# Routing of a top-2-of-8 expert layer: another operand held in the router and in the row selection, and the row scale and bias applied inside the expert items

## The chip, the cores and the metric

The kernel runs on one core of one Trainium2 chip. The metric is the device time of one execution in microseconds (us). TensorE (PE), VectorE (DVE), ScalarE (ACT), GpSimd (POOL) and the DMA queues of SyncE (SP), ACT and POOL are written by hand, engine by engine, and are held in order by semaphores alone.

## What is computed

Two batches of 256 tokens with 1024 channels go through two encoder layers with shared weights. Each layer is a token mixer, a layer norm, a channel mixer and another layer norm. The channel mixer of the second layer is the one that matters here:

```
x = layer_norm(ALPHA * x + mix, ln1_g, ln1_b)
logits = x @ w_router + b_router            # 8 experts
top_v, top_i = lax.top_k(logits, 2)
top_w = softmax(top_v)
f = sum over the two experts e:  top_w[e] * (silu(x @ w_g[e]) * (x @ w_u[e])) @ w_d[e]
x = layer_norm(ALPHA * x + f, ln2_g, ln2_b)
```

All arithmetic is float32. A float32 product is made of three products of rounded parts: high by high, high by low, low by high. The parts are tiles such as `ewhi` and `ewlo`; ACT rounds the high part and DVE subtracts it from the raw value to get the low one.

## The kernel before, in words

The 512 tokens are four tiles of 128 rows, `X[:, tt, :]`. In `out_rows(2, ...)` DVE closes the layer norm of the token mixer tile by tile: residual, statistics, `rstd` by ACT (L506), reciprocal, and the normalisation at L852, which counts `ln_norm`. Rows are normalised there, but the norm's scale and bias (`lngb`) are not applied yet.

**Routing.** PE turns the tiles to features by channel, two tiles at a time (`transposes(3)`, L1266). ACT (`xt_full`, L539) and DVE (L1003) move them to `xt32` and apply scale and bias by channel; each has half of the eight channel blocks of each half of the tokens. The router (L1476) holds 128 channels by 128 tokens of `xt32` and streams the 8 columns of the router weights `wrt`, 32 products. Beside that the rows themselves get scale and bias: POOL (`affine`, L1178, L1179) for tiles 0 and 1, DVE (`row_affine`, L816, L814) for tiles 2 and 3. ACT then rounds the rows to `xrh` (L686), DVE makes `xrl` (`x_low`, L1012).

DVE takes the logits (L1028), finds the two best experts, makes the 0/1 table `both`; PE counts places in each expert's queue (L1483 to L1486); DVE makes `sel` (L1055), a 0/1 matrix that picks the 128 rows of the first item, then the rows' places in memory `ridx` (L1071) and the list of items `tab` (L1080). POOL scatters the rows to memory by `ridx` (L1231, eight indirect DMAs), and multiplies `X` by ALPHA for the residual (L1237).

**Items.** An item is up to 128 rows of one expert; there are 11. Its weights come as 17 pieces of 1 MB (two of 0.75 MB) through a ring of six raw slots `eraw`. Fifteen of the pieces are split by ACT (`e_split`, L697) and DVE (`e_low`, L1019) into three slots of `ewhi` and `ewlo`; SP loads a slot again once `e_low` has read it. Pieces 0 to 10 make gate and up (`hidden_tanh` on ACT, `hidden_rows` on DVE L1099 and L1103, `hidden_features` on PE L1521, `hidden_high` and `hidden_low`), pieces 11 to 16 the way down. The first item's rows never go through memory: 64 products (L1496) of a 128 by 128 block of `xrh` or `xrl`, held, with the 128 columns of `sel` give them as features at once. ACT (`xg_high`, L715) and DVE (`xg_low`, L1092) split these to `xgh` and `xgl`. Later items load their rows from memory (`load_rows`, L706, which waits until all rows are scattered) and PE turns them (L1509). Within an item ACT's order around this is: split of the next item's piece 0, `xg_high`, `y_out(0)`, splits of its pieces 1 and 2, `y_out(1)`, the store of the results. Every loop runs all its engines through the same 11 items.

At the end POOL gathers the two results of each row, DVE adds them to `X` (L1138) and the last norm closes.

Of the kernel before, what the change touches and what calls it, by code (L numbers as in the profile page):

```python
# [25 lines left out]
F32 = mybir.dt.float32  # L26
# [8 lines left out]
P = 128  # L35
# [103 lines left out]
def build_trunk(nc, x0, x1, dense_w, expert_gu, expert_dn, consts, slots, vecs, mix, lnrow, wr, br, xd, yd, y0, y1):  # L139
    ctx = ExitStack()  # L140
    with ctx:
# [91 lines left out]
        slot_no = at("slot_no", [P, CAP], F32)  # L233
        assert here() <= nc.sbuf_usable_end, here()
# [8 lines left out]
        top[0] = o_xth + 2 * KD * TOK * 4  # L243
        lg = at("lg", [P, TT, NE], F32)
# [76 lines left out]
        x_scaled = sem("x_scaled")  # L321
# [79 lines left out]
        def _(sp):  # L401
# [13 lines left out]
            def ln_rows(n):  # L415

                if n == 3:
                    sp.wait_ge(x_affine_v, TT + 2)
                    sp.wait_ge(x_affine, TT + 2)
                elif n == 2:  # L420
# [36 lines left out]
            for p in range(NPC):  # L457
# [3 lines left out]
                if p == ERING - 1:  # L461
                    sp.dma_start(slot_no[:, :], slots).then_inc(in_slots, 16)
                    ln_rows(3)
# [27 lines left out]
        def _(act):  # L491
# [42 lines left out]
            def xt_full():  # L534

                for h in range(2):
                    for k in (0, 1, 4, 5):
                        act.wait_ge(xt_tr, n_tr(3, h, k))
                        nc.scalar.activation(xt32[:, k, h * SEQ:(h + 1) * SEQ], xt_bank(3, h, k), ACT.Identity,  # L539
                                             scale=vcol(1, V_L1G + k), bias=vcol(1, V_L1B + k)).then_inc(xt_full_a, 1)  # L540
# [96 lines left out]
            for L in range(DEPTH):  # L637
# [43 lines left out]
            for tt in range(TT):  # L681
                if tt < 2:
                    act.wait_ge(x_affine, TT + tt + 1)
                else:
                    act.wait_ge(x_affine_v, TT + tt - 1)
# [13 lines left out]
            for o in range(ESPL):  # L699
                e_split(o, 0)  # L700
# [38 lines left out]

            xg_high(0)  # L740
# [39 lines left out]
        def _(dve):  # L780
# [217 lines left out]
            for i, c in enumerate((C_ONE, C_TRI)):  # L998
                V.tensor_copy(ones16[:, i, :], cst[:, c:c + P])
            for h in range(2):  # L1000
                for k in (2, 3, 6, 7):
                    dve.wait_ge(xt_tr, n_tr(3, h, k))
                    V.tensor_scalar(xt32[:, k, h * SEQ:(h + 1) * SEQ], xt_bank(3, h, k), vcol(1, V_L1G + k),  # L1003
# [649 lines left out]
```

## Time and profile before

| | us |
|---|---|
| median of 3 runs (1688.52 to 1689.79) | 1689.69 |
| the profiled execution | 1689.56 |
| its span, first to last instruction | 1687.7 |
| PE busy in the span | 1598.7 (95%) |
| DVE busy | 1157.8 (69%) |
| ACT busy | 774.9 (46%) |
| POOL busy | 198.4 (12%) |

The span has three parts: dense work to 1036 us; the routing from there to the first product of the first item at 1082.94 us; then the items and the closing norm. The page's line of slices shows DMA engines at 9 tenths or more in nearly every slice of the items and at 1 to 5 tenths in most slices before them.

### The profile page before, as it was taken

What the parts mean: (1) busy time and instruction counts of PE and PEld (TensorE: products, weight loads), DVE (VectorE), ACT (ScalarE), POOL (GpSimd) and SP (SyncE); (2) the same over time, 40 slices, a digit from 0 to 9 for tenths busy, and PEclk for the clock granted to TensorE, in tenths of its full rate; (3) what the DMA queues carried; (4) which work ended last, traced back from release to release, by engine and by line L of the source; (5) the groups of instructions that cost most, each with busy time, mean ns of one, the idle gap of its engine ahead of it and who ended that gap; (6) DMA issues with size and microseconds to landing.
All of it is one profiled execution on the core that took longest, in us unless ns stands there. A gap on an engine that the chain in (4) does not pass through costs nothing.

```text
span 1687.7 us, 20082 instructions
## 1 busy us (share of the span) xinstructions
PE 1598.7 (95%) x7383; PEld 1282.7 (76%) x7383; DVE 1157.8 (69%) x1312; ACT 774.9 (46%) x990; POOL 198.4 (12%) x122
## 2 busy tenths in 40 slices
PE   7999999999999999999999998899999999999990
PEld 6877778888888888887777787777777777777770
DVE  6888747584444423579886667678877788877786
ACT  5344442252222222444443422366766667666661
POOL 0400006060000000005000242400000000000006
PEclk9999999999999999999999998699999999999995
DMA  5232222225454332222122342689999999999994
GB/s 205 75 100 75 75 101 92 95 84 199 167 184 141 115 100 97 76 88 99 67 73 77 111 150 89 230 298 357 384 357 352 354 358 354 385 351 348 353 341 162
DMA packets 134381, 325.71 MB, mean 193 GB/s; under 512 B 7984, under 2 KB 19632, under 8 KB 133808
## 3 DMA queue, kind: packets, MB, share of 16 engines
q1 hardware_dynamic: 125584, 292.36, 49.2%
q0 software_dynamic: 5296, 19.92, 3.0%
q10 hardware_dynamic: 3440, 12.58, 1.9%
q8 instruction: 41, 0.67, 0.2%
q14 instruction: 20, 0.16, 0.0%
HBM read 300.20 MB, written 24.64 MB: 192 GB/s over the span
## 4 chain that ended last, share of the span: by engine, by line
PE 73%; DMA 13%; DVE 6%; ACT 4%; issue 4%; ACTq 0%; SPq 0%; POOL 0%; DVEq 0%
PE bank L1273 15%; PE bank L1274 14%; PE bank L1275 14%; DMA eraw<-expert_gu 12%; PE bank L1312 4%; PE bank L1311 4%; PE bank L1313 4%; PE bank L1542 3%; PE bank L1544 3%; PE bank L1543 3%; ACT ewhi L697 3%; PE bank L1549 2%; DVE ewlo L1019 2%; PE bank L1385 1%; PE bank L1398 1%
## 5 line engine op out<-in xcount | busy, mean ns | idle before, releaser
L1019 DVE TENSOR_TENSOR ewlo<-eraw,ewhi 128x2048 fp32r<-128x2048 f32 x168 | 384.8, 2291 | 115.0 <-ACT ewhi L697 114.9
L1273 PE MATMUL bank<-xth,whi 128*128 128x512 f32 (+1 forms) x976 | 381.3, 391 | 1.9 <-DVE wlo L788 1.9
L788 DVE TENSOR_TENSOR wlo<-raw,whi 128x1024 fp32r<-128x1024 f32 x170 | 239.1, 1410 | 207.4 <-ACT whi L501 207.1
L697 ACT ACTIVATE ewhi<-eraw 128x2048 fp32r<-128x2048 f32 x168 | 321.7, 1916 | 122.2 <-DMA eraw<-expert_gu 73.5
L1274 PE MATMUL bank<-xtl,whi 128*128 128x512 f32 (+1 forms) x976 | 370.7, 380 | 0.0
L1275 PE MATMUL bank<-xth,wlo 128*128 128x512 f32 (+1 forms) x976 | 370.5, 380 | 0.0
L501 ACT ACTIVATE whi<-raw 128x1024 fp32r<-128x1024 f32 x170 | 178.5, 1051 | 137.1 <-PE bank L1313 123.9
L1273 PEld LDWEIGHTS bank<-xth,whi 128*128 128x128 f32 x976 | 184.1, 189 | 50.8 <-issue 8.5
L1274 PEld LDWEIGHTS bank<-xtl,whi 128*128 128x128 f32 x976 | 184.1, 189 | 36.6 <-issue 3.8
L1275 PEld LDWEIGHTS bank<-xth,wlo 128*128 128x128 f32 x976 | 184.0, 189 | 35.2
L1542 PE MATMUL bank<-ewhi,xgh 128*128 128x512 f32 (+1 forms) x528 | 205.3, 389 | 1.6 <-DVE xgl L1092 1.6
L1544 PE MATMUL bank<-ewhi,xgl 128*128 128x512 f32 (+1 forms) x528 | 197.2, 373 | 0.0
L1543 PE MATMUL bank<-ewlo,xgh 128*128 128x512 f32 (+1 forms) x528 | 196.8, 373 | 0.0
L1542 PEld LDWEIGHTS bank<-ewhi,xgh 128*128 128x128 f32 x528 | 99.9, 189 | 20.1 <-issue 4.2
L1543 PEld LDWEIGHTS bank<-ewlo,xgh 128*128 128x128 f32 x528 | 100.0, 189 | 18.7 <-issue 2.4
L1544 PEld LDWEIGHTS bank<-ewhi,xgl 128*128 128x128 f32 x528 | 99.7, 189 | 18.1
L876 DVE SCALAR_TENSOR_TENSOR cv<-hpad,vec,cv 128x512 f32<-128x512 f32 x120 | 89.9, 750 | 3.1
L562 ACT ACTIVATE gates<-bank,hvec 128x512 f32<-128x512 f32 x48 | 33.0, 688 | 126.2 <-PE bank L1275 126.2
L1542 PE MATMUL bank<-ewhi,hth 128*128 128x512 f32 x176 | 75.4, 429 | 0.0
L1241 POOL DMA_INDIRECT yg<-item_results,ridx x8 | 8.4, 1044 | 551.5 <-ACTq L767 549.3
L1220 POOL TENSOR_TENSOR mrg<-mrg 128x512 f32<-128x512 f32 x16 | 27.7, 1734 | 362.0 <-DVE mrg L973 362.0
L1544 PE MATMUL bank<-ewhi,htl 128*128 128x512 f32 x176 | 68.9, 391 | 0.0
(226 smaller groups left out, 2223.1 us busy)
## 6 DMA issues: line engine op xcount, KB each, us to landing
eraw<-expert_gu SPq DMA_DIRECT2D x124, 1024.0 KB, 9.2
raw<-dense_w SPq DMA_DIRECT2D x170, 512.0 KB, 3.4
eraw<-expert_dn SPq DMA_DIRECT2D x44, 1024.0 KB, 11.1
eraw<-expert_dn SPq DMA_DIRECT2D x22, 768.0 KB, 10.1
item_rows<-zero POOLq DMA_DIRECT2D x8, 1024.0 KB, 4.8
rows<-item_rows ACTq DMA_DIRECT2D x11, 512.0 KB, 6.8
item_results<-yrows ACTq DMA_DIRECT2D x11, 512.0 KB, 7.8
lngb<-lnrow SPq DMA_DIRECT2D x4, 1024.0 KB, 5.2
```

Source lines behind the costliest of these rows:

```text
L501: nc.scalar.activation(whi[:, g % SPL, :], raw[:, g % RAW, :], ACT.Copy).then_inc(hi_done, 1)
L697: nc.scalar.activation(ewhi[:, o % ESPL, 0:n], eraw[:, p % ERING, 0:n], ACT.Copy).then_inc(e_hi, 1)
L788: V.tensor_tensor(wlo[:, g % SPL, :], raw[:, g % RAW, :], whi[:, g % SPL, :], ALU.subtract).then_inc(lo_done, 1)
L876: ins = V.scalar_tensor_tensor(acc, src, w, acc, ALU.mult, ALU.add)
L1019: V.tensor_tensor(ewlo[:, o % ESPL, 0:n], eraw[:, p % ERING, 0:n], ewhi[:, o % ESPL, 0:n], ALU.subtract).then_inc(e_lo, 1)
L1273: mm(out, wh, xh, start=first, stop=False)
L1274: mm(out, wh, xl, start=False, stop=False)
L1275: return mm(out, wl, xh, start=False, stop=last)
L1311: mm(out, ah[:, k, t], wh, start=(k == 0), stop=False)
L1542: mm(out, ah[:, k, :], wh, start=(k == 0), stop=False)
L1543: mm(out, ah[:, k, :], wl, start=False, stop=False)
L1544: ins = mm(out, al[:, k, :], wh, start=False, stop=(k == last - 1))
```

## The change: what it does

1. **Router.** The 8 columns of `wrt` are held and 256 tokens of `xt32` are streamed, 16 products. The logits lie with experts on partitions, ACT copies them to SBUF (`lgt`), and four PE transposes turn them. ACT moves all eight channel blocks of the first token half and four of the second; DVE four of the second.
2. **Rows.** No row gets scale and bias before the items. `xrh`, `xrl` and the scattered rows are the normalised rows. POOL's `affine` and DVE's `row_affine` of this norm are gone, and POOL's multiplication by ALPHA.
3. **Selection.** `sel` is held and 512 columns of `xrh` and `xrl` are streamed, 16 products, which give the first item's rows as rows. ACT copies them to `rows`, and PE turns them as in the later items.
4. **Scale and bias** come back in `xg_high`, in every item: eight activations of 128 by 128 to a new tile `xg32`, then the rounding from there.
5. **Residual base.** ALPHA times scale and bias of `X` is done on DVE, eight operations of 128 by 1024, inside the first item, which DVE now has ahead of its loop.
6. **Order on DVE.** All of `x_low` stands before the logits; of the first three `e_low` one stands after `tab` and before `ridx`, two after `xg_low(0)`.
7. The last norm's `lngb` is loaded by POOL once the residual base is done.

```diff
-                    ln_sqrt(2)
-                    xt_full()
+                    ln_sqrt(2, range(TT - 1))
+                    xt_full(0, (0, 1, 2))
+                    ln_sqrt(2, (TT - 1,))
+                    xt_full(0, (3, 4, 5, 6, 7))
+                    xt_full(1, (0, 1, 4, 5))
...
+            e_split(0, 0)
+            act.wait_ge(rt_logit, 1)
+            nc.scalar.activation(lgt[0:NE, :], bank[0][0:NE, :], ACT.Copy).then_inc(rt_lgt, 1)
...
             def xg_high(j):
+                if not isinstance(j, int):
+                    act.wait_ge(xg_lo, j * 2)
                 for q in range(2):
                     act.wait_ge(rows_tr, j * 2 + (q + 1))
-                    nc.scalar.activation(xgh[:, 4 * q:4 * q + 4, :], quarters(bank[B_XG[q]][:, :]),
+                    for k in range(4 * q, 4 * q + 4):
+                        last = nc.scalar.activation(xg32[:, k, :], bank[B_XG[q]][:, (k % 4) * CAP:(k % 4 + 1) * CAP],
+                                                    ACT.Identity, scale=vcol(1, V_L1G + k), bias=vcol(1, V_L1B + k))
+                    last.then_inc(xg_full, 1)
+                    act.wait_ge(xg_full, j * 2 + (q + 1))
+                    nc.scalar.activation(xgh[:, 4 * q:4 * q + 4, :], xg32[:, 4 * q:4 * q + 4, :],
                                          ACT.Copy).then_inc(xg_hi, 1)
...
+            for c in range(2):
+                act.wait_ge(sel_mm, c + 1)
+                nc.scalar.activation(rows[:, 512 * c:512 * c + 512], bank[B_Y[c]][:, :], ACT.Copy).then_inc(rows_own, 1)
             xg_high(0)
...
+            def residual_base(i):
+                tt, part = i // 2, i % 2
+                if i == 0:
+                    dve.wait_ge(scattered, 16 * 2 * TT)
...
+                if part == 0:
+                    step(V.scalar_tensor_tensor(x, x, ALPHA, lngb[:, 0, :], ALU.mult, ALU.mult))
+                else:
+                    V.scalar_tensor_tensor(x, lngb[:, 1, :], ALPHA, x, ALU.mult, ALU.add).then_inc(x_base, 1)
...
+            def item(j, first=False):
                 for p in range(N_GUP):
                     if p % 2 == 1 or p == 10:
                         hidden_rows(p // 2, j)
                     if p % 2 == 0 and 2 <= p < 10:
                         hidden_low(p // 2 - 1, j)
                     e_low(p + ESPL, j)
+                    if first and p >= 6:
+                        residual_base(p - 6)
                 e_low(14, j)
+                if first:
+                    for i in range(5, 8):
+                        residual_base(i)
                 e_low(0, j + 1)
                 xg_low(j + 1)
...
             transposes(3)
+            for h in range(2):
+                pe.wait_ge(xt_full_a, (8, 12)[h])
+                if h == 1:
+                    pe.wait_ge(xt_full_b, 4)
+                cols = slice(h * SEQ, (h + 1) * SEQ)
+                for k in range(KD):
+                    ins = mm(bank[0][0:NE, cols], wrt[:, k, :], xt32[:, k, cols], start=(k == 0), stop=(k == KD - 1))
+            ins.then_inc(rt_logit, 1)
+            pe.wait_ge(rt_lgt, 1)
             for tt in range(TT):
-                for k in range(KD):
-                    ins = mm(bank[0][:, tt * NE:(tt + 1) * NE], xt32[:, k, tt * P:(tt + 1) * P], wrt[:, k, :],
-                             start=(k == 0), stop=(k == KD - 1))
+                ins = nc.tensor.transpose(bank[1][:, tt * NE:(tt + 1) * NE], lgt[0:NE, tt * P:(tt + 1) * P],
+                                          cst[0:NE, C_ID:C_ID + NE])
...
-            for k in range(KD):
+            for c in range(2):
                 for tt in range(TT):
                     for part in (xrh, xrl):
-                        ins = mm(bank[B_XG[k // 4]][:, (k % 4) * CAP:(k % 4 + 1) * CAP], part[:, tt, k * P:(k + 1) * P],
-                                 sel[:, tt, :], start=(tt == 0 and part is xrh), stop=(tt == TT - 1 and part is xrl))
-                if k % 4 == 3:
-                    ins.then_inc(rows_tr, 1)
+                        ins = mm(bank[B_Y[c]][:, :], sel[:, tt, :], part[:, tt, 512 * c:512 * c + 512],
+                                 start=(tt == 0 and part is xrh), stop=(tt == TT - 1 and part is xrl))
+                ins.then_inc(sel_mm, 1)
...
+            pe.wait_ge(rows_own, 2)
+            turn_rows()
```

The order of DVE's instructions shows points 2 and 6. First the kernel before, from the casts of two constant tiles (`ones`) to the table of the two best experts (`pick`); then the changed kernel, from the same moves to `xt` on.

```order
L999 CAST ones_126<-cst 128x128 x2
L1003 TENSOR_SCALAR xt_64<-bank,vec 128x256 x8
L816 TENSOR_TENSOR X<-X,lngb 128x1024
L814 TENSOR_TENSOR X<-X,lngb 128x1024
L816 TENSOR_TENSOR X<-X,lngb 128x1024
L814 TENSOR_TENSOR X<-X,lngb 128x1024
L1012 TENSOR_TENSOR xrl<-X,xrh 128x1024 x2
L1019 TENSOR_TENSOR ewlo<-eraw,ewhi 128x2048 x2
L1028 TENSOR_TENSOR lg<-brt,bank 128x32
```

```order
L1013 TENSOR_SCALAR xt_64<-bank,vec 128x256 x4
L1018 TENSOR_TENSOR xrl<-X,xrh 128x1024 x4
L1031 CAST ones_128<-cst 128x128 x2
L1034 TENSOR_TENSOR lg<-brt,bank 128x32
L1037 MAX mx_110<-lg 128x8 x4
```

Ahead of the logits (`lg`) four row operations, four moves to `xt` and two low parts of weights are gone, and two more `xrl` stand there; the casts stand behind them.

In the first item DVE of the changed kernel has the residual base between the low parts of the weights (`ewlo`) and the hidden blocks (`eb`, `eh`):

```order
L1025 TENSOR_TENSOR ewlo<-eraw,ewhi 128x2048
L1103 SCALAR_TENSOR_TENSOR X<-X,lngb 128x1024
L1111 SCALAR_TENSOR_TENSOR eb<-eb,bank 128x256
L1115 SCALAR_TENSOR_TENSOR eh<-eb,bank 128x256
L1025 TENSOR_TENSOR ewlo<-eraw,ewhi 128x2048
L1105 SCALAR_TENSOR_TENSOR X<-lngb,X 128x1024
L1120 TENSOR_TENSOR htl<-bank,hth 128x256
L1025 TENSOR_TENSOR ewlo<-eraw,ewhi 128x2048
L1103 SCALAR_TENSOR_TENSOR X<-X,lngb 128x1024
L1111 SCALAR_TENSOR_TENSOR eb<-eb,bank 128x256
```

The rows with `X` are new there; three of them stand ahead of the fifth hidden block and five ahead of the sixth.

On ACT the changed kernel has, from the splits of the first pieces to the end of the first item's input:

```order
L697 ACTIVATE ewhi<-eraw 128x2048
L701 ACTIVATE lgt<-bank 8x512
L697 ACTIVATE ewhi<-eraw 128x2048 x2
L706 ACT_TABLE_LOAD
L706 ACTIVATE etmp<-etmp 128x4
L752 ACTIVATE rows<-bank 128x512 x2
L721 ACTIVATE xg_104<-bank,vec 128x128 x4
L725 ACTIVATE xgh<-xg_104 128x512
L721 ACTIVATE xg_104<-bank,vec 128x128 x4
L725 ACTIVATE xgh<-xg_104 128x512
```

Before, the two `xgh` stood alone behind `etmp`, each read from PSUM; the copies to `rows`, the `xg_104` (the tile `xg32`) and the copy to `lgt` are new.

## Rows read from the trace of the kernel before

**Rows 1.** Busy time by window: us, PE, PEld, DVE, ACT, POOL, PE clock, DMA share, GB/s.
```profile
1056.00:1126.00 70.00, 62.18 (x296) 52.95 (x296) 50.34 (x83) 35.60 (x33) 21.49 (x12) 0.79 0.71 250
...
1096.00:1106.00 10.00, 9.95 (x45) 7.68 (x44) 9.80 (x9) 7.59 (x8) 4.28 (x2) 1.00 1.02 380
...
1156.00:1606.00 450.00, 435.97 (x1970) 337.15 (x1969) 358.67 (x290) 302.09 (x274) 0.00 (x0) 1.00 0.98 359
```

**Rows 2.** One window of the selection with PE alone: us, PE, clock, DMA share, GB/s.
```profile
1070.00:1072.00 2.00, 2.00 (x12) 0.50 0.29 119
```

**Rows 3.** Timeline of PE in the routing: start, us, instruction, idle before and its releaser.
```profile
1036.07 1.91 PE L1266 MATMUL bank<-cst,X 128*128 128x128 f32 x16
1041.07 3.39 PE L1266 MATMUL bank<-cst,X 128*128 128x128 f32 x16 [3.09 <-DVE X L852]
1047.57 13.18 PE L1476 MATMUL bank<-wrt,xt 128*128 128x8 f32 x64 [3.12 <-DVE xt L1003]
...
1063.85 0.25 PE L1486 MATMUL bank<-both,ones 128*128 128x8 bf16 x4
...
1082.94 0.79 PE L1542 MATMUL bank<-ewhi,xgh 128*128 128x512 f32 x1 [1.63 <-DVE xgl L1092]
```

**Rows 4.** Chain that ended last, routing and second item: start, us, what.
```profile
1067.43 13.90 PE bank L1496 x64
...
1083.73 0.43 PE bank L1543
...
1174.09 2.59 PE bank L1549 x6
```

**Rows 5.** Timeline of DVE, routing and first item.
```profile
1040.94 4.68 DVE L999 CAST ones<-cst 128x128 bf16<-128x128 f32 x2
...
1061.35 0.18 DVE L1028 TENSOR_TENSOR lg<-brt,bank 128x32 f32<-128x32 f32 x1
...
1063.61 2.35 DVE L1012 TENSOR_TENSOR xrl<-X,xrh 128x1024 fp32r<-128x1024 f32 x2
...
1066.17 1.11 DVE L1055 TENSOR_SCALAR sel<-slot_no,pos,both 128x128 fp32r<-128x128 f32 x4
...
1070.58 2.28 DVE L1019 TENSOR_TENSOR ewlo<-eraw,ewhi 128x2048 fp32r<-128x2048 f32 x1
...
1089.26 2.29 DVE L1019 TENSOR_TENSOR ewlo<-eraw,ewhi 128x2048 fp32r<-128x2048 f32 x1 [6.59 <-ACT ewhi L697]
```

**Rows 6.** Timeline of ACT, routing and first item (ACTq: its DMA queue).
```profile
1038.82 1.92 ACT L539 ACTIVATE xt<-bank,vec 128x256 f32<-128x256 f32 x4
...
1051.66 1.06 ACT L686 ACTIVATE xrh<-X 128x1024 fp32r<-128x1024 f32 x1 [2.62 <-DVE X L814]
...
1081.35 0.60 ACT L715 ACTIVATE xgh<-bank 128x512 fp32r<-128x512 f32 x1 [6.23 <-PE bank L1496]
...
1095.92 0.38 ACTq L706 DMA_DIRECT2D rows<-item_rows  x1
```

**Rows 7.** Timeline of ACT, end of the second item.
```profile
1182.14 1.91 ACT L697 ACTIVATE ewhi<-eraw 128x2048 fp32r<-128x2048 f32 x1 [2.46 <-PE bank L1544]
1184.85 1.92 ACT L697 ACTIVATE ewhi<-eraw 128x2048 fp32r<-128x2048 f32 x1 [0.80 <-DMA eraw<-expert_gu]
```

**Rows 8.** Single lines over the whole run: durations in ns min/median/max, first and last start.
```profile
L852 DVE TENSOR_SCALAR X<-X,mv,rstd x12: 811/814/1866, 331.9 to 1039.1; 128x1024 f32<-128x1024 f32 x12
...
L1138 DVE SCALAR_TENSOR_TENSOR X<-yg,mixk,X x8: 1285/1285/3245, 1656.7 to 1674.4; 128x1024 f32<-128x1024 f32 x8
...
L730 ACT ACTIVATE ht<-bank x22: 253/310/370, 1118.4 to 1632.8; 128x256 f32<-128x256 f32 x11, 128x128 f32<-128x128 f32 x11
...
L1509 PE MATMUL bank<-cst,rows x88: 270/272/273, 1122.1 to 1633.2; 128*128 128x128 f32 x88
```

**Rows 9.** The scatters on POOL: the line, and the instruction that waits for them.
```profile
L1231 POOL DMA_INDIRECT item_rows<-X,ridx x8: 947/952/2545, 1069.8 to 1080.3; - x8
...
1088.11 12.17 POOL L1237 TENSOR_SCALAR X<-X 128x1024 f32<-128x1024 f32 x4 [6.86 <-DMA item_rows<-X,ridx]
```

More of the change, by code:

```diff
@@ L243, in build_trunk @@
         top[0] = o_xth + 2 * KD * TOK * 4
+        lgt = at("lgt", [P, TOK], F32)
         lg = at("lg", [P, TT, NE], F32)
@@ L532, in xt_evac, with xt_full @@
                             nc.scalar.activation(xth[:, k, cols], xs[:, i % 4, :], ACT.Copy).then_inc(xt_hi, 1)
[L534 to L540, printed above, removed]
+            def xt_full(h, ks):
+                for k in ks:
+                    act.wait_ge(xt_tr, n_tr(3, h, k))
+                    nc.scalar.activation(xt32[:, k, h * SEQ:(h + 1) * SEQ], xt_bank(3, h, k), ACT.Identity,
+                                         scale=vcol(1, V_L1G + k), bias=vcol(1, V_L1B + k)).then_inc(xt_full_a, 1)
             def proj_out(L, m):
@@ L1080, in _ @@
             V.tensor_copy(tab[:, :], tabf[:, :]).then_inc(rt_tab, 1)
-            e_low(2, 0)
+            e_low(0, 0)
+            step(V.scalar_tensor_tensor(row[:, :, :], begin.unsqueeze(1).broadcast_to([P, TT, NE]), float(CAP),
+                                        pos[:, :, :], ALU.mult, ALU.add))
+            for k in range(2):
+                step(V.tensor_tensor(rtmp[:, :, :], row[:, :, :], pick[:, k], ALU.mult))
+                step(V.tensor_reduce(rowk[:, k, :], rtmp[:, :, :], AX.X, ALU.add))
+            V.tensor_copy(ridx[:, :, :], rowk[:, :, :]).then_inc(rt_row, 1)
             dve.wait_ge(rt_e, 1)
@@ L1113, in _ @@
             turns = dve.value_load(tab[0:1, 16:17], min_val=NE, max_val=MAX_ITEMS)
-            xg_low(0)
-            with dve.Fori(0, turns) as j:
+            def item(j, first=False):
                 for p in range(N_GUP):
@@ L1126, in _ @@
                 e_low(2, j + 1)
+            xg_low(0)
+            e_low(1, 0)
+            e_low(2, 0)
+            item(0, True)
+            with dve.Fori(1, turns) as j:
+                item(j)
             final = sem("final_step")
@@ L1232, in _ @@
                         ap=ridx[:, k, tt:tt + 1], axis=0), in_=X[:, tt, :], in_offset=None).then_inc(scattered, 16)
-            pool.wait_ge(scattered, 16 * 2 * TT)
-            pool.wait_ge(xr_lo, TT)
-            for tt in range(TT):
-                G.tensor_scalar(X[:, tt, :], X[:, tt, :], ALPHA, None, ALU.mult).then_inc(x_scaled, 1)
+            pool.wait_ge(x_base, TT)
+            pool.dma_start(lngb[:, :, :], lnrow[3:4].broadcast_to([P, 2, D])).then_inc(in_ln3, 16)
             pool.wait_ge(all_stored, 1)
@@ L1507, in rows_to_features @@
                     pe.wait_ge(rows_in, j * 16 + 16)
-                    for k in range(KD):
-                        ins = nc.tensor.transpose(bank[B_XG[k // 4]][:, (k % 4) * P:(k % 4 + 1) * P],
-                                                  rows[:, k * P:(k + 1) * P], ident)
-                        if k % 4 == 3:
-                            ins.then_inc(rows_tr, 1)
+                    pe.wait_ge(xg_full, j * 2 + 2)
+                    turn_rows()
                 def hidden_features(b):
```

89 lines of the change are left out of this document (37 added, 52 removed).

## The prediction

> **What bounds the kernel now.** I read the windows first, to see where time can be won at all. From 1156 to 1606 us the DMA engines are busy 0.98 of the time and PE 436 of 450 us [rows 1]: the items run at the pace at which weights arrive and are used. The turning of the rows (L1509), 8 per item, goes from 1122.1 to 1633.2 us in 11 items [rows 8], so ten steps of about 51 us. Nothing in the change makes an item lighter; an earlier first item moves all that follows by the same amount, a later one too. From 1056 to 1126 us the DMA engines are busy only 0.71 [rows 1], so some 20 us of transfer time lie unused there, and an earlier start finds room.
>
> The timeline of PE then gives the stage that the change rebuilds: 1036.07 us (first tiles turned) to 1082.94 us (first product of the first item), with holes of 3 us before the second half of the tiles, before the router and after it [rows 3]. The chain that ended last runs through DVE's casts and row operations, the logits, and the 64 selection products, 13.90 us [rows 4]. These are all at half clock: the granted clock is 0.50 (1.2 GHz) in a window in which PE never stopped [rows 2].
>
> **The new path, step by step**, to the new start of the first item.
>
> *Second half of the tiles.* The norm of tile 3 begins at 1039.15 us and takes 1.87 us; the others take 0.81 [rows 8]. POOL multiplies rows at that moment, which is gone afterwards, so I take 0.81: PE turns tiles 2 and 3 from 1040.0 instead of 1041.07. That takes 1.91 us (first half, full clock) or 3.39 (second half, half clock) [rows 3]; I take 1.91, as the hole before it shrinks from 3.1 to 2.0 us: 1041.9.
>
> *Router.* ACT now moves eight blocks of the first half, at 0.48 us each [rows 6]: three before the last `rstd`, five behind it from 1038.9, so to 1041.3. The other eight are shared with DVE and are ready while PE does the first half. The price of 16 products of 256 float32 columns is not in the trace; the nearest row is three of 512 float32 columns in 2.59 us at full clock [rows 4], 0.43 for 256, so 6.9 us in all at full and 13.8 at half clock. I take 7.7, two of them at half clock, since these are streamed columns and not 8-column products: the end is 1049.6. The old router took 13.18 us [rows 3] and ended at 1060.75.
>
> *Logits.* The copy to `lgt` is taken as the 0.60 us of a 512-column PSUM read on ACT [rows 6]; four transposes at 0.2 us (half clock, 3.39 over 16), handoffs 0.1: logits start at 1051.1. ACT is there in time: four `xrh` at 1.06 us [rows 6] and one split at 1.92 [rows 7] end near 1049.2. DVE's four `xrl` (2.35 us per two) end at 1049.1. The two casts behind them took 4.68 us before [rows 5], beside POOL; with POOL idle I take 0.4, and keep 2.7 us (their end at 1053.8) for the range.
>
> *Selection matrix.* From the logits to the end of `sel` it was 1061.35 to 1067.28 us. In it the two `xrl` run 1063.61 to 1065.96 [rows 5] while the counts are ready at 1064.10 [rows 3]. They now stand earlier, so 1.86 us go: 4.1 instead of 5.9, and the selection starts at 1055.4.
>
> *Selection.* 16 products of 512 columns at 0.43 us (half clock, first products of the first item [rows 4]) are 6.9 us, at full clock half that. In the first item the clock rose after six such products. I take 5.3, bounds 3.5 and 6.9. End: 1060.7.
>
> *From there to the first item.* Before: `xgh` 0.60, `xgl` and handoff 1.0 [rows 3, 6]. Now a copy to `rows` 0.65, four transposes 0.6, eight activations, two roundings of 0.6, handoffs 0.2, then the same 1.0. One activation of 128 columns: 0.48 for 256 [rows 6] less the 0.12 by which a copy of 128 is shorter than one of 256 (253 and 370 ns [rows 8]), 0.36, so 2.9. Together 6.5: **the first item starts at 1067.2 instead of 1082.94, 15.7 us earlier.**
>
> **What the first item gives back.** DVE is busy 9.80 of 10 us there [rows 1], so what is added cannot lie in holes. The two `e_low` that move behind `xg_low(0)` (2 x 2.29) fit the 6.59 us that DVE idles at the item's start [rows 5]. The eight operations of the residual base are taken as L1138, the same operation and size: 1.30 us with handoff [rows 8]. Three stand ahead of the fifth hidden block and five ahead of the sixth, and PE needs both before it can turn them and go on: 6.5 us. DVE runs ahead of PE by 1.7 us: the first low part ends at 1091.55 [rows 5], and PE can use it only after 36 products, from 1093.2. So 4.8 us stay. Bounds: nothing, if DVE can catch up in time, and all eight, 10.4 us. The last three lie where DVE waits for weights (358.67 of 450 us busy in the steady items [rows 1]).
>
> **Every later item** costs ACT 3.0 us more (eight activations and handoffs). It stands ahead of the splits of pieces 1 and 2, before which ACT idles 2.46 and 0.80 us [rows 7], 3.26 together; the second ends by a DMA. So nothing, but with 0.3 us to spare. The scale and bias rows that POOL and DVE lost were on the chain and are counted above; the multiplication by ALPHA on POOL ran beside the first item and is worth nothing. The load of the last `lngb` moves from SP to POOL's queue, with the whole of the items to land.
>
> **Sum:** -15.7 + 4.8 = -10.9 us against the profiled 1689.56 us (the median is 1689.69): **1678.7 us**.
>
> **Rivals.**
> *Scatters.* They started 13.1 us ahead of the first item and had landed 18.3 us after their start [rows 9]; `load_rows` follows 13.0 us into the item [rows 6]. By the order above they now start near 1061.2, 6.0 us ahead, and land 12.3 us into it: just in time. One of the eight took 2.55 us where the median is 0.95 [rows 9], and a low part of weights ran on DVE then. If three meet one, they land 4.1 us late for ACT, of which PE has about 1 us in hand: 3.1 us more, 1681.8. The Trainium skill, "SBUF — State Buffer", section "Who interferes with whom", has a DVE operation with two SBUF inputs contend with a POOL operation that reads SBUF, but finds descriptor generation not held up by such an operation; by that this rival costs nothing, and the row of 2.55 us speaks against it.
> *The residual base in full*, 10.4 us: 1684.3. For it: DVE's 9.80 of 10 us. *Swallowed*: 1673.9.
> *Half clock throughout.* The router ends at 1043.4 + 13.8 = 1057.2, 7.6 us later, and the selection takes 1.6 more: 1687.9, no change that a measurement tells. For it: back-to-back products did not lift the clock before [rows 2]; against it, products of 512 columns did, within the first item. The Trainium skill, "TensorE: Matmul & The Clock Gate", section "What's actually happening", has sustained activity lift the clock; by that alone the old selection would have run at full clock, which the 0.50 contradicts.
> *The stream sets the end*, whatever the first item does: 1689.6. Against it the 20 us of unused DMA time, more than 10.9.
> *Longer items: slower.* If an activation of `xg32` costs more than 0.40 us, the splits behind come late and with them the next loads, in ten items. At 0.53 us the gain of 10.9 is used up; at 0.60, 4.9 us per item, it is 1.6 x 10 - 10.9 = 5 us slower, about 1695. Against it: 0.36 as worked out, and PE needs pieces 1 and 2 later than ACT ends them.
>
> **How the numbers follow.** Forecast 0.50; scatters 0.15; residual in full 0.12; swallowed 0.12; half clock 0.04; stream 0.03; longer items 0.04. A measurement of this kernel tells about 0.2%, 3.4 us, from no change. The first four are faster by more than that: 0.89; half clock and stream 0.07; slower 0.04. The range goes from the case of nothing given back, 1673.5, to the residual in full with 1 us more, 1685.5, which also takes in casts that stay slow (2.7) and a selection at half clock (1.6) beside the forecast.
>
> **What would show it.** Right: the router as 16 products in 7 to 9 us, the selection in about 5, the first product of the first item near 1067, turnings of rows (L1527 now) first 44 us behind it instead of 39, then 51 us apart, DVE without a hole in the middle of the first item, PE idle there before the fifth and sixth hidden blocks. Wrong: ACT waiting for the scatters before its load of rows; steps between the items above 51 us; products of 0.86 us in the whole router; a first item that begins after 1072.

## The result, and the profile after

The changed kernel takes **1680.48 us** (median of 5 runs, 1678.43 to 1682.19) against 1689.5 us (5 runs, 1688.52 to 1689.79) for the kernel before on the same chip: ratio 0.9949, 95% interval 0.9937 to 0.996. It is faster by about 9 us; 1678.7 was forecast, and the range of 1673.5 to 1685.5 holds the result. The profiled execution, the fastest of the five, took 1678.43 us; its span is 1676.6 us.

Two windows of the changed kernel, the first item and the steady items (us, then busy time of PE, PEld, DVE, ACT and POOL, PE clock, DMA share, GB/s), answer to [rows 1]:

```profile
1056.00:1126.00 70.00, 60.71 (x259) 46.74 (x258) 55.54 (x54) 41.47 (x50) 10.75 (x9) 0.94 0.82 299
1156.00:1606.00 450.00, 436.51 (x1963) 336.72 (x1963) 359.00 (x291) 328.48 (x346) 0.00 (x0) 1.00 0.98 359
```

The steady stage is what it was: the DMA engines at 0.98, the same 359 GB/s. ACT does 26.4 us more there, its eight activations per item, and PE does not notice. The first window now has more weights in it (299 GB/s, 250 before), as the items start earlier.

The timeline of PE answers to [rows 3]:

```profile
1033.99 1.91 PE L1285 MATMUL bank<-cst,X 128*128 128x128 f32 x16
1037.95 1.97 PE L1285 MATMUL bank<-cst,X 128*128 128x128 f32 x16 [2.05 <-DVE X L865]
1039.84 7.07 PE L1496 MATMUL bank<-xt,wrt 128*8 128x256 f32 x32
1047.59 0.41 PE L1500 MATMUL bank<-cst,lgt 8*128 8x8 f32 x4 [0.68 <-ACT lgt L701]
...
1052.37 0.77 PE L1520 MATMUL bank<-xrh,sel 128*128 128x512 f32 x1 [1.60 <-DVE sel L1057]
...
1058.45 0.39 PE L1520 MATMUL bank<-xrl,sel 128*128 128x512 f32 x1
1059.53 1.09 PE L1527 MATMUL bank<-cst,rows 128*128 128x128 f32 x8 [0.69 <-ACT rows L752]
1065.57 0.79 PE L1573 MATMUL bank<-ewhi,xgh 128*128 128x512 f32 x1 [4.95 <-DVE xgl L1092]
```

This execution came to the first row 2.08 us earlier than the profiled one before (1036.07). The routing has no part in that: the issues of the third `lngb` load, 90 us ahead of it, already stand 1.94 us apart (944.05 here, 945.99 before). In the eleven later runs the first row lies between 1034.72 and 1035.90; why all twelve come there earlier than the one trace of the kernel before, by 1.1 us on average, is open. So I count from that row. From there to the first product of the first item it was 46.87 us and is **31.58 us, 15.3 us less**; from that product to the turning of the second item's rows it was 39.2 us and is **44.69 us, 5.5 us more**; the ten steps between turnings took 510.3 us and take 511.7, **1.4 more**; and from the last turning to the end it is 54.6 us instead of 55.3. The last turning of the kernel before, then two of the changed kernel, that of the third item's rows and the last:

```profile
1632.42 1.04 PE L1509 MATMUL bank<-cst,rows 128*128 128x128 f32 x8
```

```profile
1162.99 1.03 PE L1527 MATMUL bank<-cst,rows 128*128 128x128 f32 x8
...
1621.98 1.03 PE L1527 MATMUL bank<-cst,rows 128*128 128x128 f32 x8
```

Together -15.3 + 5.5 + 1.4 - 0.7 = -9.1 us; the medians differ by 9.0. That they agree so closely is partly luck. In this execution the second half of the tiles and the router ran at full clock. In six of the ten later traces with the same code up to there they did so only in part, and the selection begins 20.0 us after the first row instead of 18.4. PE in the same window of the changed kernel, then of the run with the residual spread (us, busy, granted clock, DMA share, GB/s):

```profile
1040.00:1046.80 6.80, 6.80 (x32) 1.00 0.00 0
```

```profile
1040.00:1046.80 6.80, 6.80 (x31) 0.75 0.00 0
```

Where the first item gives time back is seen in PE's next rows:

```profile
1095.50 0.43 PE L1552 MATMUL bank<-cst,eh 128*128 128x128 f32 x2 [1.26 <-DVE eh L1115]
...
1103.42 0.43 PE L1552 MATMUL bank<-cst,eh 128*128 128x128 f32 x2 [1.86 <-DVE eh L1115]
...
1107.27 0.33 PE L1552 MATMUL bank<-cst,eh 128*128 128x128 f32 x1 [0.53 <-DVE eh L1115]
...
1110.26 1.03 PE L1527 MATMUL bank<-cst,rows 128*128 128x128 f32 x8
```

DVE makes the hidden blocks late, three times, 3.65 us in all, and here is what stands ahead of them (DVE, with two rows of the routing):

```profile
1046.47 0.35 DVE L1031 CAST ones<-cst 128x128 bf16<-128x128 f32 x2
1048.04 0.19 DVE L1034 TENSOR_TENSOR lg<-brt,bank 128x32 f32<-128x32 f32 x1 [1.21 <-PE bank L1500]
...
1093.24 1.22 DVE L1103 SCALAR_TENSOR_TENSOR X<-X,lngb 128x1024 f32<-128x1024 f32 x1
1094.50 0.42 DVE L1111 SCALAR_TENSOR_TENSOR eb<-eb,bank 128x256 f32<-128x256 f32 x1
1094.95 0.42 DVE L1115 SCALAR_TENSOR_TENSOR eh<-eb,bank 128x256 f32<-128x256 f32 x1
...
1097.49 1.22 DVE L1105 SCALAR_TENSOR_TENSOR X<-lngb,X 128x1024 f32<-128x1024 f32 x1
...
1101.16 1.22 DVE L1103 SCALAR_TENSOR_TENSOR X<-X,lngb 128x1024 f32<-128x1024 f32 x1
...
1105.41 1.22 DVE L1105 SCALAR_TENSOR_TENSOR X<-lngb,X 128x1024 f32<-128x1024 f32 x1
1106.55 0.28 DVE L1111 SCALAR_TENSOR_TENSOR eb<-eb,bank 128x128 f32<-128x128 f32 x1
...
1109.26 1.22 DVE L1103 SCALAR_TENSOR_TENSOR X<-X,lngb 128x1024 f32<-128x1024 f32 x1
```

One operation of the residual base is 1.22 us. One stands ahead of the fourth hidden block, three ahead of the fifth and four ahead of the sixth (1106.55); the fifth operation (1109.26) comes behind it, where the section on the change and the prediction count it in front. The other part is the clock. Windows of PE alone (us, busy, granted clock, DMA share, GB/s): the selection, the way from it to the first item, the first item's start and what follows:

```profile
1052.40:1056.40 4.00, 4.00 (x10) 0.50 0.00 0
...
1060.00:1065.00 5.00, 0.62 (x6) 0.97 1.03 413
1066.00:1071.00 5.00, 5.00 (x13) 0.50 0.96 307
1072.00:1074.00 2.00, 2.00 (x11) 1.00 0.95 328
```

The selection begins at half clock (1.2 GHz) and reaches the full one only for its last products. Then PE is busy 0.62 of 5 us, while ACT scales the first item's input, and the item begins at half clock again: some 13 products, 5.7 us, pass before the rise. In the kernel before it was six. The forecast had some half-clock products in the selection, too few, and none at the item's start beyond those of the kernel before.

### The profile page after: what moved, and what is told of

The parts are those of the page before. It is cut to its first block, busy times and chain, and to the rows that moved or that the text cites. A ratio compares the mean times of both kernels' runs of the same rounds, so it can differ in the third digit from the quotient of the medians.

```text
span 1676.6 us, 20036 instructions
## 1 busy us (share of the span) xinstructions
PE 1584.8 (95%) x7315; PEld 1261.0 (75%) x7315; DVE 1156.1 (69%) x1312; ACT 813.8 (49%) x1093; POOL 177.5 (11%) x115
## 4 chain that ended last, share of the span: by engine, by line
PE 72%; DMA 13%; DVE 6%; ACT 4%; issue 4%; ACTq 0%; SPq 0%; POOL 0%; DVEq 0%
PE bank L1292 15%; PE bank L1293 14%; PE bank L1294 14%; DMA eraw<-expert_gu 11%; PE bank L1331 4%; PE bank L1330 4%; PE bank L1332 4%; PE bank L1573 3%; PE bank L1575 3%; PE bank L1574 3%; ACT ewhi L697 3%; PE bank L1580 2%; DVE ewlo L1025 2%; PE bank L1404 1%; PE bank L1417 1%
## 5 line engine op out<-in xcount | busy, mean ns | idle before, releaser
L1575 PEld LDWEIGHTS bank<-ewhi,xgl 128*128 128x128 f32 x528 | 100.1, 190 | 18.4
L1574 PE MATMUL bank<-ewlo,hth 128*128 128x512 f32 x176 | 68.7, 390 | 0.0
L1332 PE MATMUL bank<-whi,hl 128*128 128x512 f32 x176 | 68.5, 389 | 0.0
```

Source lines behind the costliest of these rows:

```text
L1332: return mm(out, al[:, k, t], wh, start=False, stop=(k == 2 * per - 1))
L1574: mm(out, ah[:, k, :], wl, start=False, stop=False)
L1575: ins = mm(out, al[:, k, :], wh, start=False, stop=(k == last - 1))
```

## The experiments

My theory after this: the give-back is the residual base (about 4 us) and the clock (1 to 2 us). Rivals: the scatters, ACT's eight activations, DVE's loop.

| run | median us | ratio to the kernel before |
|---|---|---|
| no residual base | 1671.52 (one run) | |
| residual spread | 1675.36 | 0.9923 (0.9909 to 0.9937) |
| PE kept busy | 1681.37 | 0.9962 (0.9948 to 0.9976) |
| no scale and bias in the items | 1683.96 (one run) | |
| old router | 1684.97 (one run) | |
| old selection | 1683.78 (one run) | |
| PE kept busy, rows loaded later | 1676.26 | 0.993 (0.9913 to 0.9946) |
| the same, residual spread | 1671.78 | 0.9904 (0.9887 to 0.992) |
| changed kernel, `lngb` loaded last | 1677.83 | 0.9938 (0.9925 to 0.9952) |
| all four together | 1670.19 | 0.9891 (0.9876 to 0.9906) |
| all four, scaling shared with DVE | 1670.34 | 0.9893 (0.9878 to 0.9909) |

The changed kernel itself stands at 0.9949 (0.9937 to 0.996). Where a run's interval overlaps with that, what tells the two apart is their traces, one of each.

**Without the residual base.** ALPHA, scale and bias of the residual are left out. The load of the last `lngb`, which had waited for them, then goes once all scatters have landed, in the first item.

```diff
-                    if first and p >= 6:
-                        residual_base(p - 6)
...
-                if first:
-                    for i in range(5, 8):
-                        residual_base(i)
...
-            pool.wait_ge(x_base, TT)
+            pool.wait_ge(scattered, 16 * 2 * TT)
+            pool.wait_ge(in_ln, 16 * 3)
```

> Leaves out the residual's ALPHA, scale and bias (eight operations on DVE in the first item). In the changed kernel the first item takes 44.7 us from its first product to the turning of the next rows, 39.2 before. Theory: 3.7 of the 5.5 us are PE waiting for hidden blocks behind the residual base on DVE (1.26, 1.86 and 0.53 us before L1552), the rest is half clock at the start of the item. Then this kernel shows 41.0 us, none of these three waits, and about 3.7 us less in all. Rival: the two low parts of weights that moved behind the first item's input, or the later loads, hold the item; then it stays at 44 to 45 us.

The first product of the first item begins at 1065.75 us; PE's rows behind it:

```profile
1088.43 0.43 PE L1547 MATMUL bank<-cst,eh 128*128 128x128 f32 x2 [0.21 <-DVE eh L1115]
...
1106.21 1.03 PE L1522 MATMUL bank<-cst,rows 128*128 128x128 f32 x8
```

40.46 us from first product to turning, 4.2 less than 44.69, and of the three waits one of 0.21 us is left. The residual base costs 4.2 us. What remains over the 39.2 us of the kernel before, 1.3 us, is there without it. The whole fell by more than the 3.7 us expected: the median by 9.0, the span of the profiled execution by 6.9, of which 2.9 are the ten steps (508.85 us instead of 511.72). In this run POOL issues the `lngb` load at 1080.30, not at 1116.64.

**Residual spread** over the first four items, two operations each, at their ends.

```diff
-                    if first and p >= 6:
-                        residual_base(p - 6)
...
-                    for i in range(5, 8):
-                        residual_base(i)
+                    residual_base(2 * j)
...
+                    residual_base(2 * j + 1)
...
-            item(0, True)
-            with dve.Fori(1, turns) as j:
+            for i in range(TT):
+                item(i, True)
+            with dve.Fori(TT, turns) as j:
```

> The same eight operations, two in each of the first four items, where DVE waits for ACT in every item (before the low part of the next item's piece 0, and behind the low parts of its input). Theory: these holes, 2.5 and 2.3 us, take one operation of 1.22 us each, so the first item is as short as without them (41 us) and items two to four stay near 51 us: 3.5 us faster than the changed kernel, about 1677 us. Rival: DVE has no true hole there, each operation is paid in its item, and the total stays at about 1680 us.

The first item takes 40.59 us, as good as without the residual base. The ratio falls from 0.9949 to 0.9923, some 4.4 us, about what the residual base had cost (the two intervals touch). But one thing was new: the step from the turning of the second item's rows to that of the third's, 52.73 us in the changed kernel, is 51.13 here, and the one from the fifth's to the sixth's is 54.04. A long step had moved with the end of the residual base. I come back to it.

**PE kept busy.** Products on the rows, whose results nobody reads, 6 before the counts, 5 after them and 14 behind the turning of the first rows:

```diff
+            def keep_busy(n):
+                for _i in range(n):
+                    mm(bank[2][:, :], xrh[:, 0, 0:P], xrh[:, 0, 0:512], start=True, stop=True)
+            pe.wait_ge(xr_hi, TT)
+            keep_busy(6)
...
+            keep_busy(5)
...
+            keep_busy(14)
```

> 25 idle products of 512 columns into an unused bank, 6 behind the turned logits, 5 behind the counts, 14 behind the turned rows, where PE waits. Theory: the clock is at half for 5.3 us of the selection and 5.9 us of the first item because PE was idle before; with the holes filled both run at full clock: selection 3.7 instead of 6.5 us, first item 3 us shorter, 5 us faster in all, about 1675 us. Rival: the clock does not follow such short fillings, or the idle products run at half clock and stand in the way: no gain, or up to 3 us slower.

The clock is 1.00 in the selection, on the way from it and at the item's start (PE: us, busy, clock, DMA share, GB/s):

```profile
1053.00:1057.00 4.00, 3.64 (x28) 1.00 0.02 4
1060.00:1064.00 4.00, 4.00 (x22) 1.00 0.91 307
1066.00:1071.00 5.00, 5.00 (x24) 1.00 0.96 306
```

The selection takes 3.97 us. Yet the first item takes 49.25 us and the kernel is no faster, and ACT shows why:

```profile
1083.08 0.38 ACTq L709 DMA_DIRECT2D rows<-item_rows  x1
1083.63 1.91 ACT L697 ACTIVATE ewhi<-eraw 128x2048 fp32r<-128x2048 f32 x1 [6.20 <-DMA item_rows<-X,ridx]
```

The load of the second item's rows has to wait until all scatters have landed; the split of the next weights is behind it in ACT's order, and 5 us of PE go:

```profile
1087.92 0.80 PE L1582 MATMUL bank<-ewhi,xgh 128*128 128x512 f32 x1 [5.04 <-DVE ewlo L1025]
```

This is the rival of the scatters, where it had not decided before. The last scatters of this run:

```profile
1063.48 0.95 POOL L1252 DMA_INDIRECT item_rows<-X,ridx  x1 [0.30 <-issue]
...
1070.89 2.83 POOL L1252 DMA_INDIRECT item_rows<-X,ridx  x1 [0.30 <-issue]
1074.03 2.69 POOL L1252 DMA_INDIRECT item_rows<-X,ridx  x1 [0.30 <-issue]
```

**No scale and bias in the items.** ACT rounds straight from PSUM, as before; scale and bias are left out.

```diff
-                    for k in range(4 * q, 4 * q + 4):
-                        last = nc.scalar.activation(xg32[:, k, :], bank[B_XG[q]][:, (k % 4) * CAP:(k % 4 + 1) * CAP],
-                                                    ACT.Identity, scale=vcol(1, V_L1G + k), bias=vcol(1, V_L1B + k))
...
+                    nc.scalar.activation(xgh[:, 4 * q:4 * q + 4, :], quarters(bank[B_XG[q]][:, :]),
```

> Leaves out the scale and bias of the items' rows: ACT rounds from PSUM as before the change, DVE subtracts from PSUM. Theory: the eight activations cost 3.0 us on the way to the first item (6.7 us from the last selection product to the first product of the item become 3.6) and nothing in the later items, whose step stays at 51.1 us. Rival: they also hold the later items; then ten steps of the turning become shorter by 1 to 20 us in all.

From the second copy to `rows` to the first product it is 3.51 us instead of 6.69: ACT's activations cost 3.2 us on that path (2.9 forecast). The item then starts at full clock, ACT waits 7.61 us for the scatters, and the first item takes 51.12 us: in this one run the kernel is slower, though it does less.

```profile
1064.98 0.49 PE L1568 MATMUL bank<-ewhi,xgh 128*128 128x512 f32 x1 [1.76 <-DVE xgl L1087]
```

The later steps begin with 52.70, 51.57 and 50.92 us, those of the changed kernel with 52.73, 51.61 and 51.00; all ten take 510.9 us instead of 511.7. So the activations cost the later items nothing that stands out from what differs between executions.

**Old router**, with the rest as changed (128 columns of `xt32` held, 8 streamed):

```diff
...
-                    ins = mm(bank[0][0:NE, cols], wrt[:, k, :], xt32[:, k, cols], start=(k == 0), stop=(k == KD - 1))
...
+                    ins = mm(bank[1][:, tt * NE:(tt + 1) * NE], xt32[:, k, tt * P:(tt + 1) * P], wrt[:, k, :],
+                             start=(k == 0), stop=(k == KD - 1))
...
```

> The changed kernel with the old router alone: 32 products that hold the tokens and stream 8 columns, logits with tokens on partitions at once, no copy to lgt and no turning. Theory: the router takes 13.2 us again instead of 7.1, the copy and the turning (1.1 us) are saved, so the selection starts about 5 us later after the turning of the first tiles (18.4 us in the changed kernel, 23.4 here) and the whole is 5 us slower. Rival: at full clock the 32 products are quicker, half of 13.2, since PE has had less idle time before; then nothing is lost.

```profile
1042.12 13.66 PE L1493 MATMUL bank<-wrt,xt 128*128 128x8 f32 x64
```

The selection starts 24.27 us after the first row of the routing, 18.38 in the trace of the changed kernel and 20.0 in the six told of above: the streamed router, with its copy and its turning back, is worth 5.9 or 4.3 us (5 expected). The rival, 32 quicker products at full clock, did not come: from 1042.30 to 1055.70 us PE is busy throughout at a granted clock of 0.50. So part of what streaming is worth is the clock that came with it.

**Old selection**, with the rest as changed (features at once, no copies and no turning):

```diff
...
-                        ins = mm(bank[B_Y[c]][:, :], sel[:, tt, :], part[:, tt, 512 * c:512 * c + 512],
...
+                        ins = mm(bank[B_XG[k // 4]][:, (k % 4) * CAP:(k % 4 + 1) * CAP], part[:, tt, k * P:(k + 1) * P],
+                                 sel[:, tt, :], start=(tt == 0 and part is xrh), stop=(tt == TT - 1 and part is xrl))
...
```

> The changed kernel with the old selection alone: 64 products that hold the rows and stream 128 columns of the selection matrix, features at once, no copy to rows and no turning for the first item; scale and bias as in the changed kernel. Theory: 13.9 us again instead of 6.5, less 1.3 us of copy and turning: the first item starts 6 us later. But the scatters then have 6 us more until the first item needs them. So 6 us slower in all. Rival: the first half of the features is scaled while the second is selected, so that 2 us more are hidden: 4 us slower.

First product 37.08 us after the first row instead of 31.58: 5.5 us, of which some 1.6 are transposes of the second half that ran at half clock in this run (3.55 us instead of 1.97). So the streamed selection itself is worth about 4 us, the rival's figure and not the 6 us of the theory.

**PE kept busy, rows loaded later.** ACT loads the second item's rows at the eighth piece instead of the fourth, behind the splits that PE needs first.

```diff
-                    if p == 3:
+                    if p == 7:
                         act.wait_ge(scattered, 16 * 2 * TT)
```

> The idle products of the third run, and the load of the next item's rows moved from ACT's fourth place in the item to its eighth, some 12 us later. In the third run the clock stayed full but ACT stood 6.2 us before that load, waiting for the scatters, and PE lost 5.0 us. Theory: with the load behind, the 5 us of the clock come out: first item 41.5 us instead of 49, about 1675 us. Rival: the weights are late as well when the item starts full speed (the ring had only one slot reloaded ahead), so ACT waits for DMA in place of the scatters, and the first item stays above 44 us.

ACT no longer waits; 42.7 us from first product to turning. The two waits for `eh` of 1.38 and 1.84 us are left. Against 44.69 the full clock is worth 2.0 us inside the item. The one edit takes the ratio of the kept-busy kernel from 0.9962 to 0.993: what the clock had won, the wait for the scatters had eaten.

**The same, residual spread.**

> The run before with the residual base spread over four items as in the second run. Theory: the gains add, 3.7 us more than the run before, about 1671 us, and the first item takes 38 us. Rival: with both gone the weights bound the first item; then it stays above 40 us and the gain over the second run is under 2 us.

```profile
1063.96 0.49 PE L1582 MATMUL bank<-ewhi,xgh 128*128 128x512 f32 x1 [1.59 <-DVE xgl L1092]
...
1101.78 1.03 PE L1535 MATMUL bank<-cst,rows 128*128 128x128 f32 x8
```

37.8 us, 4.9 less than with the residual base in the first item. But the step from the turning of the fifth item's rows to that of the sixth's is 54.15 us. Its window (columns as in the first fence), beside that of the step ahead of it:

```profile
1203.34:1254.30 50.96, 49.67 (x224) 38.25 (x223) 43.27 (x36) 37.24 (x40) 0.00 (x0) 1.00 0.99 361
1254.33:1308.40 54.07, 51.27 (x224) 39.38 (x223) 43.48 (x36) 36.99 (x40) 0.59 (x1) 0.97 1.00 364
```

The engines do the same work at the same rate of transfers, and 54.07 x 364 is 19.7 MB where 50.96 x 361 is 18.4. What POOL does in it, 0.59 us, is the issue of the last norm's `lngb`, 1 MB. In the changed kernel it stands here:

```profile
1068.51 1.89 POOL L1252 DMA_INDIRECT item_rows<-X,ridx  x1 [0.30 <-issue]
1116.64 0.59 POOL L1256 DMA_DIRECT2D lngb<-lnrow  x1 [46.24 <-DVE X L1105]
```

It is issued when the residual base is done, in the middle of the stream. But DVE enters its loop in the same items, so that had to be told apart.

**`lngb` loaded last**, by SP behind the last weights; nothing else changes.

```diff
-            pool.wait_ge(x_base, TT)
-            pool.dma_start(lngb[:, :, :], lnrow[3:4].broadcast_to([P, 2, D])).then_inc(in_ln3, 16)
...
+            sp.wait_ge(x_base, TT)
+            sp.dma_start(lngb[:, :, :], lnrow[3:4].broadcast_to([P, 2, D])).then_inc(in_ln3, 16)
```

> The changed kernel with one edit: the 1 MB load of the last norm's scale and bias is issued by SP after the last piece of weights, not by POOL when the residual base is done. In the changed kernel the turning of the second item's rows and that of the third lie 52.7 us apart, the next two 51.6, the later ones 50.9. Load theory (the transfer takes its time from the weight stream, which bounds the items): the 52.7 becomes 51.0 to 51.6, and the median falls by 1 to 2.5 us from 1680.5. Loop theory (DVE and the other engines enter their loop there, and the load is hidden): the 52.7 stays within 0.3 and the median within 0.7. The first item is as before the edit under both, 44 to 45 us.

The turnings of the second and third items' rows:

```profile
1110.19 1.03 PE L1527 MATMUL bank<-cst,rows 128*128 128x128 f32 x8
...
1161.16 1.03 PE L1527 MATMUL bank<-cst,rows 128*128 128x128 f32 x8
```

50.97 us; 52.73 in the changed kernel. The ten steps are 509.3 us instead of 511.7, and the median is 2.6 us lower (by the ratios 1.9, with intervals that overlap). The first item is the same, 44.5 us. The load theory holds and that of the loop falls, since the loop was not touched. That it is the time of the load and not POOL's queue agrees with the run without the residual base, where POOL issued it in the first item and no step is above 51.52. The next step stays at 51.57 us (51.61 in the changed kernel); what makes it 0.7 us longer than the later ones is open.

**All four together:** residual spread, PE kept busy, rows loaded later, `lngb` last.

> The combination of the residual base spread over four items, the filler products that hold the clock, and the rows loaded later by ACT (1671.8 us), with the load of the last norm's scale and bias moved behind the weights. There the one long step lies between the fourth and the fifth item, 54.2 us, where both the load falls and DVE enters its loop. Load theory: that step becomes 51 to 51.5 and the median 1668.3 to 1669.5. Loop theory: the step stays at 54 and the median at 1671 to 1672.5.

The step of 54.15 us is 51.19, as the load theory has it. The median, 1670.19, is 0.7 us above the range expected. In the profiled execution the transposes of the second half took 2.99 us instead of 1.97 and the router 7.67 instead of 7.07, which the trace of the run before did not have; and the step from the second item's rows to the third's is 51.92 us, 51.13 there, for a reason that is open.

**Scaling shared with DVE**, four of the first item's eight blocks (ACT's other four are left out):

```diff
...
+            dve.wait_ge(rows_tr, 2)
+            dve.wait_ge(xg_full, 1)
+            for k in range(4, 8):
+                last = V.tensor_scalar(xg32[:, k, :], bank[B_XG[1]][:, (k % 4) * CAP:(k % 4 + 1) * CAP],
+                                       vcol(1, V_L1G + k), vcol(1, V_L1B + k), ALU.mult, ALU.add)
```

> As the combination with the load behind the weights, and DVE instead of ACT scales the second half of the first item's input, four operations of 128 by 128 beside ACT's four. If ACT's eight activations stand on the path to the first product, the first item's first product comes 1 to 1.8 us earlier than in that combination and the median falls by as much, to 1667 to 1668; if the rows of the second item or the stream take it back, the median is the same within 0.6 us.

A miss. From the second copy to `rows` to the first product it is 6.0 us instead of 6.6, and the median is the same. One counter serves both halves, so DVE waits for ACT's four before its own begin (1.03 us in its timeline): they follow one another, not beside one another. That a version with two counters would win more was not tried. The fastest by its ratio is that of all four, 1.1% under the kernel before.

## Why the prediction was right, step by step

*Second half of the tiles.* 3.96 us after the first row, 3.93 forecast: the normalisation of tile 3 took 0.81 us without POOL, and the transposes ran at full clock, 1.97 us. Right, in this execution; in the six others they took 2.5 to 3.6 us.

*Router.* 7.07 us against 7.7: full clock throughout, 0.44 per product, as the scaled row of 512 columns had it [rows 4]. The caution of two half-clock products was not needed in this execution, but in the six others the router took 7.1 to 8.2 us. Transposes and router together were forecast at 9.6 us; they took 9.0 here and 10.7 there, so that the profiled execution was lucky by 1.6. The half clock throughout, a rival, came in none.

*Logits and selection matrix.* The casts took 0.35 us (4.68 before [rows 5]; 0.4 forecast), and from the logits to the selection 4.33 us passed (4.3 forecast). Right.

*Selection.* 6.47 us against 5.3. "In the first item the clock rose after six such products. I take 5.3" was mis-sized: it rose after twelve. (Six products at 0.43 us and ten at half that are 4.7; the prediction does not say what the other 0.6 is.)

*From there to the first item.* 6.73 us against 6.5. Together 15.3 us earlier; 15.7 was forecast.

*What the first item gives back.* The step put the residual base at 4.8 us. It is 4.2 at the changed kernel's clock (run without it) and 4.9 at full clock (spread, in the kept-busy kernels). The mechanism, operations on DVE ahead of hidden blocks that PE waits for, is right; the size is partly luck. It counted five operations ahead of the sixth block, where four stand, at 1.30 us, where each takes 1.22, and then took off 1.7 us for DVE's lead. Four of 1.22 are 4.9, just what came at full clock, with nothing off for a lead; at the changed kernel's clock 0.7 of it did not come. So an operation too many stood against a lead that was not there. And the step left out the clock: the item begins at half clock after the idle stretch of the tail, for 5.7 us. Without a residual base in it the first item takes 37.8 us with no product at half clock (kept busy, spread), 39.2 with six (the kernel before) and 40.5 with twelve (the run without it), 0.2 us for each. That is the 1.3 us that the run without the residual base still has over 39.2.

*Later items.* The eight activations cost nothing that can be told, as forecast: without them the first steps are the same and all ten are 0.8 us shorter.

*The load of the last `lngb`* "moves from SP to POOL's queue, with the whole of the items to land". **This term failed**: I asked when the data is needed and not what runs when it is fetched. Before, SP fetched it at 1054 us, when the DMA engines had time to spare (0.43 busy, last but one in the second line):

```profile
1054.05 0.34 SPq L424 DMA_DIRECT2D lngb<-lnrow  x1
...
1054.00:1060.00 6.00, 6.00 (x30) 6.00 (x30) 5.35 (x5) 5.95 (x4) 0.00 (x0) 0.50 0.43 175
```

Now it takes 1 MB out of a stream that bounds the items, and costs 2.4 us of the ten steps (by all traces 1.6: 511.65 us on average in the eight with the load in the stream, 510.04 in the three with it at the end). 1 MB at 364 GB/s is 2.9 us by estimate; the step of 54.15 lost 3.0, the one of 52.73, earlier in the stream, 1.8. Steps above 51 us stood in the prediction as a sign of its being wrong, and this sign came.

The sum came out 1.8 us too good: 0.4 in the routing, 0.7 in the first item, and 2.4 for the load, less 1.0 by which the ten steps are shorter than before without it (509.3 against 510.3) and 0.7 at the end (by the averages 1.6 for the load and 0.2). Where these last two come from is open; they are the size of what differs from execution to execution.

*The rival of the scatters* did not decide, but was near. Three of them met low parts on DVE, and the issue of the last ended at 1070.40; in the kept-busy kernel the load of the rows could go 6.4 us after the last issue, which by estimate would be about 1076.8 here, and ACT wanted it at 1079.97. What makes the way to the item or its start faster uses these 3 us of slack up, as two runs showed, the kept-busy one and the one without scale and bias. Of the other rivals, the stream did not set the end, and longer items did not come; the residual base was neither swallowed nor there in full.

## What to carry to other kernels

In a stage that transfers bound, every byte fetched there costs its time, even if nobody waits for it (1 MB cost 1.8 to 3.0 us of a step here): move a load only into a stretch where the DMA engines idle, or behind the stream. A gain on the path to a stage can wake a wait that was covered by the slowness of that stage, so take the next wait away with it (the clock alone gained nothing here; the clock with the later load of rows gained 3 to 4 us over the changed kernel). Count in a product's price which clock it meets, and what the engine did just before: two stretches in which PE did little, ahead of the selection and ahead of the first item, were each paid for with twelve or more products at half clock.

## What the runs showed of the hardware

**The clock.** The granted clock was 1.00 (2.4 GHz) while the changed router ran in the profiled execution, behind transposes with a hole of 2 us, and its 16 products of 256 float32 columns took 7.07 us. With the same code up to there it was 0.75 to 0.81 in the same window (1040.00 to 1046.80 us) of six other traces, and 1.00 in four. I had not expected so much of it to be lost twice after that: 0.50 in most of the selection, and 0.50 again at the start of the first item, each time behind a stretch in which PE did little. With PE kept busy in these stretches it was 1.00 in both. Back-to-back products did not always lift it: the old router stayed at 0.50 for 13.4 us of unbroken work.

**Scatters beside low parts.** A scatter's issue takes 0.95 us on POOL, the first one or two of a run up to 1.09. Each one that begins while DVE subtracts a piece of weights takes 1.89 to 2.85 us, in twelve of the thirteen traces. In the thirteenth, the run with the old selection, DVE idles for 6.13 us at the same place, none begins there, and these scatters stay short. POOL of that run:

```profile
1066.13 0.95 POOL L1249 DMA_INDIRECT item_rows<-X,ridx  x1 [0.30 <-issue]
1067.39 0.95 POOL L1249 DMA_INDIRECT item_rows<-X,ridx  x1 [0.30 <-issue]
1068.65 0.95 POOL L1249 DMA_INDIRECT item_rows<-X,ridx  x1 [0.30 <-issue]
1069.91 0.95 POOL L1249 DMA_INDIRECT item_rows<-X,ridx  x1 [0.30 <-issue]
```

The Trainium skill, "SBUF — State Buffer", section "Who interferes with whom", infers that such an operation does not hold up the making of descriptors. The rows speak against it, unless what waits is the scatter's reading of its row numbers (`ridx`); that the two compete for the same port was not tested by itself.
